# One of eight channel blocks of the depthwise convolutions moved from VectorE to GpSimd

## What is computed

```
def depthwise_conv(y, w, b):          # w: 31 taps for each channel
    out = conv_general_dilated(y, w, padding=15 on both sides, one group per channel)
    return out + b

def conv_branch(h, w_in, dw, db, ln_g, ln_b, w_out):
    a, b, gate = jnp.split(h @ w_in, 3, axis=-1)
    y = a * jax.nn.sigmoid(b)
    y = depthwise_conv(y, dw, db)
    y = jax.nn.silu(layernorm(y, ln_g, ln_b))
    return (y * jax.nn.silu(gate)) @ w_out
```

## Time and profile before

| | us |
|---|---|
| median of 3 runs | 4638.64 (4631.03 to 4643.04) |
| the profiled execution | 4638.01 |
| its span, first to last instruction | 4636.2 |
| first convolution, first tap to last | 1812.77 to 2052.15 |
| second convolution, first tap to last | 4368.47 to 4536.04 |

### The profile page before, as it was taken

How to read it: one execution, slowest core, us unless ns; L and a number is a source line. 1 busy time by engine, 2 the same in 40 slices (tenths; PEclk the granted TensorE clock), 3 DMA queues, 4 the chain that set the end, 5 groups by cost and what they waited for, 6 DMA issues and landing times. The chain is left out here.

```text
span 4636.2 us, 76849 instructions
## 1 busy us (share of the span) xinstructions
PE 4028.2 (87%) x34008; PEld 2283.8 (49%) x34008; DVE 1786.7 (39%) x2909; ACT 908.5 (20%) x1548; POOL 342.0 (7%) x315
## 2 busy tenths in 40 slices
PE   5779999996999998967999777777778999999996
PEld 2334444443444445534555466766654555454432
DVE  2223444304144005983201045445423344342494
ACT  1220000000000001011000334333312343341101
POOL 0000000000000000000000323322201000010000
PEclk8779999998999999988999589999999999999998
DMA  1013333221233120201122311111101111111120
GB/s 65 12 39 127 141 131 145 91 100 54 78 147 123 69 72 28 63 36 64 71 92 74 142 58 32 37 44 42 70 4 47 60 40 50 48 30 71 55 91 18
DMA packets 74111, 319.82 MB, mean 69 GB/s; under 512 B 7328, under 2 KB 42144, under 8 KB 59488
## 3 DMA queue, kind: packets, MB, share of 16 engines
q1 hardware_dynamic: 65488, 280.86, 17.0%
q0 software_dynamic: 8336, 34.61, 2.1%
HBM read 278.75 MB, written 30.41 MB: 67 GB/s over the span
## 5 line engine op out<-in xcount | busy, mean ns | idle before, releaser
L594 PE MATMUL lin_ps<-hn,ring 128*128 128x512 f32 (+1 forms) x4320 | 1680.5, 548 | 85.5 <-DVE hn L1715 31.8
L594 PEld LDWEIGHTS lin_ps<-hn,ring 128*128 128x128 f32 x4320 | 825.6, 192 | 898.0 <-issue 850.7
L594 PE MATMUL lin_ps<-arena,ring 128*128 128x512 f32 (+4 forms) x2800 | 1137.0, 577 | 40.9 <-DVE arena L1974 24.8
L594 PEld LDWEIGHTS lin_ps<-arena,ring 128*128 128x128 f32 (+2 forms) x2800 | 541.0, 196 | 623.3 <-issue 582.5
L1269 ACT ACTIVATE arena<-lin_ps 128x512 f32<-128x512 f32 (+4 forms) x527 | 312.3, 607 | 1786.2 <-PE lin_ps L594 1784.8
L594 PE MATMUL lin_ps<-arena 64*64 64x64 f32 (+2 forms) x9728 | 503.3, 240 | 136.3 <-issue 54.4
L1715 DVE SCALAR_TENSOR_TENSOR arena<-arena,vec 128x512 f32<-128x512 f32 (+2 forms) x563 | 436.5, 853 | 149.3 <-PE lin_ps L594 148.0
L594 PEld LDWEIGHTS lin_ps<-arena 64*64 64x64 f32 (+1 forms) x9728 | 366.7, 142 | 221.4 <-issue 156.9
L594 PE MATMUL sum_ps<-arena 64*64 64x64 f32 x7136 | 301.9, 223 | 51.4 <-issue 41.8
L594 PEld LDWEIGHTS sum_ps<-arena 64*64 64x64 f32 x7136 | 256.8, 136 | 58.9 <-issue 45.9
L2304 POOL TENSOR_TENSOR hn<-hn 128x512 f32<-128x512 f32 (+1 forms) x30 | 41.7, 1389 | 2566.8 <-ACT hn L1269 2566.8
(11 more groups left out here) (174 smaller groups left out, 2734.1 us busy)
## 6 DMA issues: line engine op xcount, KB each, us to landing
arena<-w_mod SPq DMA_DIRECT2D x24, 2048.0 KB, 7.8
ring<-w_up SPq DMA_DIRECT2D x16, 2048.0 KB, 7.7
ring<-w_down SPq DMA_DIRECT2D x16, 2048.0 KB, 7.8
features<-arena POOLq DMA_DIRECT2D x64, 384.0 KB, 2.6
ring<-w_attn SPq DMA_DIRECT2D x16, 1536.0 KB, 6.6
ring<-w_conv_in SPq DMA_DIRECT2D x16, 1024.0 KB, 5.9
ring<-features SPq DMA_DIRECT2D x40, 384.0 KB, 3.7
arena<-features SPq DMA_DIRECT2D x24, 384.0 KB, 3.4
```

The lines of the kernel that those rows point to most:

```text
L594: return pe.matmul(out, lhsT, rhs, start=start, stop=stop)
```

## The change

VectorE keeps the blocks 0 to 3 and 5 to 7, as three pairs and a single one. Block 4 goes to GpSimd, with one accumulator of its own (`pacc`) and with the padded input of block 0, free by then, as scratch for the products. [...] `cmean` moves into `std`, to make room. The table NEXT has new places, and PE sums block 4 in the last place but one.

```
+        cmean = std[:, :]
+        yacc, pacc = at(24936, 2, SPAN), at(26502, SPAN)
+        BY_DVE, BY_POOL = [(0, 1), (2, 3), (5, 6), (7,)], 4
...
+                for n, k in enumerate([0, 1, 2, 3, 5, 6, BY_POOL, 7]):
+                    if k == BY_POOL:
+                        pe.wait_ge(pool_y, i + 1)
+                    else:
+                        pe.wait_ge(conv_y, 7 * i + (k if k < BY_POOL else k - 1) + 1)
+                    for c0, cw in SEGS[width]:
+                        m = mm(sum_ps[:, 256 + c0:256 + c0 + cw], ones, cy[:, k, c0:c0 + cw], n == 0, n == KD - 1)
...
-                def tap(k, t):
+                def tap(k, t, e, lag):
...
-                        dve.wait_ge(L.sem, L.n - (0 if t == TAPS - 1 and k % 2 else 1))
+                        dve.wait_ge(L.sem, L.n - lag)
...
-                NEXT = {(0, 14): 2, (0, 24): 3, (1, 4): 4, (1, 15): 5, (1, 26): 6, (2, 6): 7}
+                NEXT = {(0, 10): 2, (0, 21): 3, (1, 0): 4, (1, 10): 5, (1, 21): 6, (2, 0): 7}
...
-                        tap(2 * pair, t)
-                        tap(2 * pair + 1, t)
+                        tap(some[0], t, 0, len(some) - 1)
+                        if len(some) == 2:
+                            tap(some[1], t, 1, 0 if t == TAPS - 1 else 1)
...
+            def pool_conv(i, width):
+
+                lo, k = 0 if width == ALL else SHIFT[CTX], BY_POOL
+                y, wx = pacc[:, lo:SPAN], ypad[:, 0, lo:SPAN]
+                pool.wait_ge(glu_ready, 8 * i + k + 1)
+                pool.wait_ge(conv_y, 7 * i + 2)
+                for t in range(TAPS):
+                    x, w = ypad[:, k, lo + t:SPAN + t], V("conv_dw_2", TAPS * (8 * i + k) + t)
+                    if t == 0:
+                        o(nc.gpsimd.tensor_scalar(y, x, w, V("conv_db_2", 8 * i + k), ALU.mult, ALU.add), taps)
+                    else:
+                        pool.wait_ge(pool_tap, taps.n)
+                        o(nc.gpsimd.tensor_scalar(wx, x, w, None, ALU.mult), taps)
+                        pool.wait_ge(pool_tap, taps.n)
+                        if t < TAPS - 1:
+                            o(nc.gpsimd.tensor_tensor(y, y, wx, ALU.add), taps)
+                for c0, cw in SEGS[width]:
+                    z = SHIFT[c0]
+                    m = nc.gpsimd.tensor_tensor(cy[:, k, c0:c0 + cw], pacc[:, z:z + cw], ypad[:, 0, z:z + cw], ALU.add)
+                m.then_inc(pool_y, 1)
+
+            partial_sum("sgu", SEQ, hn)
+            partial_sum("first", SEQ, hn)
+            pool_conv(0, ALL)
+            partial_sum("rw", ALL, hn)
```

More of the change, by code:

```diff
@@ L320, in build @@
         mod_c, mod_full, mod_mm, mod_acc = sem("mod_c"), sem("mod_full"), sem("mod_mm"), sem("mod_acc")
+        pool_y, pool_tap = sem("pool_y"), sem("pool_tap")
         glu_ready, conv_y, conv_sq, conv_s = sem("glu_ready"), sem("conv_y"), sem("conv_sq"), sem("conv_s")
@@ L382, in build @@
         csb, cab = at(18792, GLU, ALL), at(21864, GLU, ALL)
-        cmean = at(24936, ALL)
-        yacc = at(25704, 2, SPAN)
+        cmean = std[:, :]
+        yacc, pacc = at(24936, 2, SPAN), at(26502, SPAN)
+        BY_DVE, BY_POOL = [(0, 1), (2, 3), (5, 6), (7,)], 4
         HPW = ALL + 4
@@ L766, in conv @@
                 linear(f"conv{i}_g", KD, 512, full_h, width, wait=(h_ready, 8 * (NI[nrm] + 1)))
[L768 to L773, removed]
+                for n, k in enumerate([0, 1, 2, 3, 5, 6, BY_POOL, 7]):
[5 more added lines that the diff above has]
+                        m = mm(sum_ps[:, 256 + c0:256 + c0 + cw], ones, cy[:, k, c0:c0 + cw], n == 0, n == KD - 1)
+                m.then_inc(conv_s, 1)
+                for k in range(KD):
+                    pe.wait_ge(conv_sq, 8 * i + k + 1)
+                    for c0, cw in SEGS[width]:
+                        m = mm(sum_ps[:, 256 + c0:256 + c0 + cw], ones, hn[:, k, c0:c0 + cw], k == 0, k == KD - 1)
+                m.then_inc(conv_s, 1)
                 linear(f"conv{i}_out", KD, 512, lambda k, c0, cw: cy[:, k, c0:c0 + cw], width, wait=(conv_out, 8 * (i + 1)))
@@ L1923, in conv @@
                 gl, done = Signal(glu_ready), Signal(conv_y)
-                gl.n, done.n = 8 * i, 8 * i
+                gl.n, done.n = 8 * i, 7 * i
                 lo = 0 if width == ALL else SHIFT[CTX]
@@ L1933, in gated @@
                     o(m, gl)
-                def tap(k, t):
+                def tap(k, t, e, lag):
                     w = V("conv_dw_2", TAPS * (8 * i + k) + t)
-                    x, y = ypad[:, k, lo + t:SPAN + t], yacc[:, k % 2, lo:SPAN]
+                    x, y = ypad[:, k, lo + t:SPAN + t], yacc[:, e, lo:SPAN]
                     if t:
-                        dve.wait_ge(L.sem, L.n - (0 if t == TAPS - 1 and k % 2 else 1))
+                        dve.wait_ge(L.sem, L.n - lag)
                     if t == 0:
@@ L1948, in tap @@
                             z = SHIFT[c0]
-                            m = stt(cy[:, k, c0:c0 + cw], ypad[:, k, z + t:z + t + cw], w, yacc[:, k % 2, z:z + cw], ALU.mult, ALU.add)
+                            m = stt(cy[:, k, c0:c0 + cw], ypad[:, k, z + t:z + t + cw], w, yacc[:, e, z:z + cw], ALU.mult, ALU.add)
                         o(m, done)
-                NEXT = {(0, 14): 2, (0, 24): 3, (1, 4): 4, (1, 15): 5, (1, 26): 6, (2, 6): 7}
+                NEXT = {(0, 10): 2, (0, 21): 3, (1, 0): 4, (1, 10): 5, (1, 21): 6, (2, 0): 7}
                 gated(0)
                 gated(1)
-                for pair in range(KD // 2):
+                for n, some in enumerate(BY_DVE):
                     for t in range(TAPS):
-                        if (pair, t) in NEXT:
-                            gated(NEXT[pair, t])
+                        if (n, t) in NEXT:
+                            gated(NEXT[n, t])
                             o.wait()
-                        tap(2 * pair, t)
-                        tap(2 * pair + 1, t)
+                        tap(some[0], t, 0, len(some) - 1)
+                        if len(some) == 2:
+                            tap(some[1], t, 1, 0 if t == TAPS - 1 else 1)
                     o.wait()
@@ L2304, in partial_sum @@
                     o(nc.gpsimd.tensor_tensor(a, a, last_cols(dst[:, k, :], width), ALU.add), partial if k == KD - 2 else None)
-            for nrm, width in ((n, ALL if n == "rw" else SEQ) for n in PARTS[:-3]):
-                partial_sum(nrm, width, hn)
+            taps = Signal(pool_tap)
+            def pool_conv(i, width):
[13 more added lines that the diff above has]
+                            o(nc.gpsimd.tensor_tensor(y, y, wx, ALU.add), taps)
+                for c0, cw in SEGS[width]:
+                    z = SHIFT[c0]
[5 more added lines that the diff above has]
+            partial_sum("rw", ALL, hn)
             pool.wait_ge(h_ready, 8 * (NI["rw"] + 1))
@@ L2365, in _ @@
             partial_sum("c1", SEQ, hn)
+            pool_conv(1, SEQ)
             partial_sum("last", SEQ, hn)
```

## The result

The changed kernel takes 4696.1 us (median of 4 runs, 4693.1 to 4700.0) against 4636.3 for the one before: ratio 1.013, 95% interval 1.0115 to 1.0145. It is 60 us slower. The forecast was 80 us slower; the result lies 0.1 us inside the lower end of its range, 4696.

What follows compares the result with a forecast made beforehand. VectorE's taps were taken to set the end of both convolution stages. GpSimd's holds less the gains gave +51.0 and +29.0, together +80.0 on 4638.0 us: 4718 us, range 4696 to 4768.

Steps and rivals of the forecast that it cites:

- the gain of 44 us: Both convolutions: what VectorE's lost block and PE's shorter last sums would save if GpSimd cost nothing, giving 4594 us.
- Neither runs while the other does: VectorE instructions with two SBUF inputs and GpSimd instructions reading SBUF exclude each other for a whole instruction.
- 29 x 1.65 + 1.4: First convolution: GpSimd's sums each hold VectorE's taps 1.65 us, the last, split one 1.4; 49.2 us in all.
- 0.9: First convolution: us that each GpSimd product holds VectorE's taps; 31 of them add 27.9 us.
- lower bound of 0.77: Least hold per product in us: VectorE's one-input pace, 0.97, less the 0.20 by which a sum's hold is shorter.
- The estimate of 0.67 us: GpSimd product at 1.03 cycles per column, 1.2 GHz; held in full, it would put the kernel near 4707 us.
- -24.8 - 1.3: First convolution's gain: 24.8 us from VectorE's taps, 1.3 us from PE summing one block instead of two at the end.
- -16.7 - 1.3: Second convolution's gain: 16.7 us from VectorE's taps, 1.3 us from PE's shorter sums at the end.
- The first rival: Consecutive VectorE taps are not held by GpSimd, so the kernel gains 44 us: 4594 us; chance 7 in 100.
- the second (GpSimd ends last): VectorE's taps keep their place, GpSimd gets in only where VectorE breaks and finishes after it: 4735 us; chance 8.
- the third: Only GpSimd's sums hold taps, since a product reads one input: 4673 us; chance 4.
- the fourth: A GpSimd product costs more than a sum, 2.5 us or more: above 4790 us; chance 4.

Runs made afterwards that it cites:

- e_sums: Changed kernel with GpSimd's products left out, its sums adding the shifted input itself: 4683.3 us, ratio 1.0083 to the kernel before.
- e_idle: Changed kernel with GpSimd doing only block 4's first tap and final sum, taps 1 to 29 left out: 4614.7 us, 0.9937 of the kernel before.
- e_late: Changed kernel with GpSimd starting block 4 only when VectorE's seven blocks are done: 4811.8 us, ratio 1.0361 to the kernel before.
- e_products: Changed kernel with GpSimd making block 4's products but no sums except the last: 4644.3 us, ratio 0.9993 to the kernel before.
- e_psum: Changed kernel with VectorE's two accumulators in PSUM, PE's sums starting when the three pairs are done: 4608.2 us, ratio 0.993 to the kernel before.
- e_twoop: Changed kernel with GpSimd's product written as times weight plus 0.0 in one instruction: 4701.3 us, ratio 1.0123 to the kernel before.

## Why the prediction was right, and where it was off

The mechanism was right in each part that decides the sign: VectorE's taps set the end of both stages; a tap with both inputs in SBUF waits while GpSimd reads SBUF; each GpSimd instruction adds its hold; the gain of 44 us is more than eaten up. Too strict was "Neither runs while the other does": it was the reading, not the record, that excluded the other engine. Taps were forecast 2.2 us apart, each of them held; they are 1.6 apart, and of three one goes free. By the rule of the Trainium skill that the prediction drew on ("SBUF — State Buffer", "Who interferes with whom"), the trace agrees for who excludes whom, memset included. It says that the loser is blocked for the whole instruction, and there the measurement differs, and decides: the product's record of 2.85 us blocks 0.65.

The terms were off, holds and gain both too large, so that the errors partly cancelled:

- "29 x 1.65 + 1.4" for the sums, 49.2 us: 1.30 each. What failed is the extrapolation from the earlier trace rows, where 1.61 was added at 768 columns. (The second of the two GpSimd instructions there, L2342, is a product of two tensors and not a sum; the sum at 2800.61 alone adds 2.54 - 0.96 = 1.58.) e_sums shows 1.30 and 1.57 for the same instruction on other operands, so that price was no constant of the form. At 512 columns 0.82 stood in place of 1.00.
- "0.9" for a product: 0.65, below my lower bound of 0.77. I derived both bounds from the lengths of records, but it is the reading that counts. The estimate of 0.67 us, which I had worked out from the cycles per column in "GPSIMD Engine Reference", section 3.1, of the Trainium skill and left out of the sum and the bounds, agrees with it.
- Holds in all: 77.1 and 47.0 forecast, 58.0 and 37.4 measured (against e_idle, whose own GpSimd instructions still hold for 1.8 in the first stage).
- "-24.8 - 1.3" and "-16.7 - 1.3": -21.1 and -13.9. Pairs (58.2) and single block (32.9) came out as worked out. Of the 5.0 us missing in the first stage 1.4 are the wait at the first gated product, 1.4 what GpSimd's remaining instructions cost (the taps last 217.3 us, and 216.0 in e_late, where GpSimd is idle until they are done), and 1.3 PE's second sums; of the 4.1 in the second, PE's are 2.0. The rest is small and lies in places that I haven't followed up.

The sum of stages is +36.9 + 23.6 = +60.5 us, and the runs say +59.8; with the scatter of the mixer the second agrees closer than it had to. The holds were 28.7 us too dear and the gain 9.1 us too large. Had the gain come out as forecast, the kernel would have taken some 4687 us, below the range: that the result lies in it is luck, the direction isn't. The first rival (no hold) falls by the single records, the second (GpSimd ends last) since it ended at 2019.9 and VectorE at 2085.1, the third by e_products and the fourth by the 0.65. That PE's waits would be 77 and 55 us in all was too much for the same reason: 58.7 and 45.1. (Where the prediction says that PE waits some 77 us longer, it means 77 in all, 51 longer.)

## What to carry to other kernels

Before a share of VectorE's elementwise work goes to GpSimd, count how many inputs each VectorE instruction beside it reads from SBUF. With two, GpSimd's reading time is added to VectorE's, and here one tap moved cost 1.95 us to save 0.92. With one of them in PSUM the same split ran almost free and turned 60 us lost into 35 to 37 gained. To price such a hold, take the columns that GpSimd reads, not the length of its record. A single input isn't always enough, though: the `tensor_scalar` of the first tap has one and was held too, 1.31 us where it takes 0.69 alone.

## What the runs showed of the hardware

- In the changed kernel the hold goes with the columns that GpSimd reads: 0.65 us for 783, 0.43 for 512, and for sums, which read two inputs, 1.30 and 0.82. That is 0.80 to 0.84 ns for a column. A second price stands beside it, 0.98 to 1.03 ns: about half of the sums in e_sums (1.57 us at 783, 1.00 at 512), the 1.58 at 768 columns in the earlier trace rows and the 1.00 at 512 in the earlier trace rows. In all of them the operands lie otherwise. I haven't tried which offset does it, so it stays open.
- A VectorE `tensor_scalar` from SBUF to SBUF, 783 columns in 0.69 us, is held by GpSimd's first tap though it has one input (e_idle, 1.31 us). Into PSUM it takes 1.09, and 1.10 beside the same instruction of GpSimd, which then takes its 1.01 (e_psum).
- On GpSimd a `tensor_scalar` with one operation takes 2.26 us for 783 columns, and with two operations (the first tap of e_late or e_psum) 1.01. In e_twoop adding 0.0 makes the product's record shorter, 1.53 us where it was 2.85. Why is open.
- Of two sums of 783 and 768 columns the longer takes 1.57 us in e_late, the other 1.81 in the earlier trace rows.
- Accumulating 783 columns in PSUM costs VectorE nothing here from the second tap on: 1.03 us a tap in e_psum. The first tap, 1.09 and not 0.69, is longer.
